# Value tiles first and by tokens, three pairs' tiles ahead of attention, three slices a step

## The reference

```python
n = rms_norm(h, attn_norm[l])
# layer 0, hybrid: 8 dilated heads (roped q, k) and 8 forgetting heads of 64
proj = n @ w_in                       # q, k, v of both kinds, and fb
logf = log_sigmoid(fb + b_f)          # the forget gate, 8 rows
o = concat(dilated_attention(rope(qa) * scale, rope(ka), va),
           forgetting_attention(qb * scale, kb, vb, logf))
h = h + o @ w_out
# layer 1, differential: 8 heads with two softmaxes and values of 128
q, k, v = split(n @ w_qkv)            # q and k roped
o = (softmax(q1 k1^T) - lam * softmax(q2 k2^T)) v
h = h + (rms_norm(o, subln_g) * (1 - lam_init)) @ w_out
```

## Time and profile before

| | before |
|---|---|
| median of 3 runs | 2503.67 us (2503.62 to 2503.73) |
| profiled execution | 2503.53 us |
| its span in the trace | 2501.6 us |
| TensorE busy | 2456.5 us (98%) |
| VectorE, ScalarE, GpSimd busy | 1568.4, 1039.2, 974.5 us |
| granted TensorE clock | 0.999 |

### The profile page before, as it was taken

The page is one execution under the profiler, slowest core; times in us unless marked ns, Lnnn a source line. Parts: engine busy times, 40 slices in busy tenths (PEclk is TensorE's granted clock), DMA queues, the critical chain, the costliest instruction groups (busy, mean ns, idle before and its releaser), DMA issues.

```text
span 2501.6 us, 33281 instructions
## 1 busy us (share of the span) xinstructions
PE 2456.5 (98%) x11238; PEld 1899.5 (76%) x11238; DVE 1568.4 (63%) x2255; ACT 1039.2 (42%) x1574; POOL 974.5 (39%) x421
## 2 busy tenths in 40 slices
PE   9999999999999999999999999999999999999998
PEld 6777888888777688888777467888877756888886
DVE  7654664777677666177678757515557876751555
ACT  5444552232344555133473654313336365431333
POOL 2232444444310044444455034444455504444443
PEclk9999999999999999999999999999999999999999
DMA  5222223232322223233222022323322202232232
GB/s 184 83 83 66 97 92 103 91 106 95 98 88 81 64 96 107 86 98 105 80 88 64 22 72 81 106 87 100 105 80 88 75 14 72 84 102 92 93 104 80
DMA packets 66510, 219.59 MB, mean 88 GB/s; under 512 B 8552, under 2 KB 8808, under 8 KB 66288
## 3 DMA queue, kind: packets, MB, share of 16 engines
q1 hardware_dynamic: 64384, 214.79, 26.9%
q10 hardware_dynamic: 2032, 3.56, 0.4%
HBM read 209.91 MB, written 2.11 MB: 85 GB/s over the span
## 4 chain that ended last, share of the span: by engine, by line
PE 87%; DVE 6%; issue 3%; ACT 3%; POOL 1%; DMA 0%; SPq 0%; DVEq 0%; POOLq 0%; ACTq 0%
PE bank_G L685 25%; PE bank_G L687 25%; PE bank_G L686 25%; PE bank_X L2442 1%; PE bank_S L1832 1%; PE bank_X L1860 1%; PE bank_O L2078 1%; PE bank_O L1846 1%; PE bank_S L2067 1%; PE bank_S L1612 1%; PE bank_S L2346 1%; PE bank_O L1622 1%; PE bank_O L2543 1%; PE bank_X L2090 0%; PE bank_X L2531 0%
## 5 line engine op out<-in xcount | busy, mean ns | idle before, releaser
L566 POOL TENSOR_TENSOR wlo<-raw,whi 128x1024 fp32r<-128x1024 f32 (+2 forms) x361 | 883.9, 2450 | 1474.3 <-ACT whi L656 1418.1
L685 PE MATMUL bank_G<-n_hi,whi 128*128 128x512 f32 x2216 | 881.2, 398 | 7.4 <-POOL wlo L566 3.2
L687 PE MATMUL bank_G<-n_hi,wlo 128*128 128x512 f32 x2216 | 863.5, 390 | 0.0
L686 PE MATMUL bank_G<-n_lo,whi 128*128 128x512 f32 x2216 | 862.9, 389 | 0.0
L656 ACT ACTIVATE whi<-raw 128x1024 fp32r<-128x1024 f32 (+2 forms) x389 | 404.3, 1041 | 676.0 <-PE bank_G L687 675.4
L685 PEld LDWEIGHTS bank_G<-n_hi,whi 128*128 128x128 f32 x2216 | 416.4, 188 | 108.9 <-issue 13.2
L687 PEld LDWEIGHTS bank_G<-n_hi,wlo 128*128 128x128 f32 x2216 | 415.9, 188 | 88.7
L686 PEld LDWEIGHTS bank_G<-n_lo,whi 128*128 128x128 f32 x2216 | 416.4, 188 | 87.4 <-issue 4.3
L685 PE MATMUL bank_G<-a_hi,whi 128*128 128x512 f32 x704 | 275.1, 391 | 0.0
L687 PE MATMUL bank_G<-a_hi,wlo 128*128 128x512 f32 x704 | 273.9, 389 | 0.0
L686 PE MATMUL bank_G<-a_lo,whi 128*128 128x512 f32 x704 | 273.9, 389 | 0.0
(11 more groups left out here) (358 smaller groups left out, 2861.6 us busy)
## 6 DMA issues: line engine op xcount, KB each, us to landing
raw<-in_w_mix_in SPq DMA_DIRECT2D x40, 512.0 KB, 3.3
raw<-in_w_hyb_in SPq DMA_DIRECT2D x25, 512.0 KB, 3.4
raw<-in_w_diff_in SPq DMA_DIRECT2D x24, 512.0 KB, 3.3
raw<-in_w_up0a SPq DMA_DIRECT2D x22, 512.0 KB, 3.3
raw<-in_w_up0b SPq DMA_DIRECT2D x22, 512.0 KB, 3.3
raw<-in_w_up1a SPq DMA_DIRECT2D x22, 512.0 KB, 3.3
raw<-in_w_up1b SPq DMA_DIRECT2D x22, 512.0 KB, 3.3
raw<-in_w_up2a SPq DMA_DIRECT2D x22, 512.0 KB, 3.3
```

Of the source, the lines that this page charges most:

```text
L566: pool.tensor_tensor(b.wlo[:, g.slot, w], b.raw[:, g.slot, w], b.whi[:, g.slot, w], ALU.subtract).then_inc(b.lo_ready, 1)
L685: pe.matmul(out, b.whi[:, g.slot, w], hi[:, hi_at + k, :], start=(k == 0), stop=False)
L686: pe.matmul(out, b.whi[:, g.slot, w], lo[:, lo_at + k, :], start=False, stop=False)
L687: mm = pe.matmul(out, b.wlo[:, g.slot, w], hi[:, hi_at + k, :], start=False, stop=(k == pieces - 1))
```

## The change

Value tiles come first in both blocks, and their products are turned around: a block of 128 tokens of `n_hi` or `n_lo` stands, 512 columns of the weights move, and the result has tokens on partitions, as attention wants it. Eight value tiles are two groups of four; each tile holds two slices of the contraction for 512 output columns, and a group accumulates over its four tiles in four banks (`value_bank`) of X, O and S. ScalarE evacuates a group into `v` (`keep_values_act`), scaled per token; for this the root is turned into a column by four small matmuls (`column`) and copied by VectorE (`keep_column_dve`). Transposes, `vst` takes, `keep_v_dve` and the posts of value tiles go. The norm's sum moves into the third tile of the hybrid block and the first of the differential one (`SUM_INSIDE`). `lead` becomes 15 (hybrid: values, q0 to k1, f, q2, k2) and 14 (differential), and `slices` 3, so that the last slice is in step 26. The forget gate's ScalarE and VectorE work moves ahead of attention. In the differential block the tile from which VectorE splits is now the 17th (before: the 15th). The host lays out the value weights to match. In `load_start` the swaps of halves of tiles 0 to 3 go, since these are value tiles now.

```diff
 def hyb_in_pe(pe, b):
-    gemm(pe, b, Index(a.g0), b.n_hi, b.n_lo, KD, lambda k: pe.wait_ge(b.nlo_ready, k + 1))
-    gemm(pe, b, Index(a.g0 + 1), b.n_hi, b.n_lo, KD, None, range(KD // 2))
-    pe.wait_ge(b.square_in, 16)
-    norm_sum(pe, b, 0)
-    gemm(pe, b, Index(a.g0 + 1), b.n_hi, b.n_lo, KD, None, range(KD // 2, KD))
+    value_tiles_pe(pe, b, a, 0, 0)
     inputs_start_pe(pe, b, a)
...
 def diff_in_pe(pe, b):
-    first_gemms_n(pe, b, ATT_DIFF.g0, 24, 2)
+    value_tiles_pe(pe, b, ATT_DIFF, 24, 2)
...
-def hyb_in_act(act, b):
+def hyb_in_act(act, b, link):
     for n in range(1, ATT_HYB.lead):
+        if n in VALUE_ENDS:
+            keep_values_act(act, b, ATT_HYB, VALUE_ENDS.index(n))
         split_hi(act, b, Index(ATT_HYB.g0 + n + 2))
+        if ATT_HYB.tiles[n - 1] == ("f", 0):
+            forget_log_act(act, b, link)
...
+VALUE_TILES, VALUE_ENDS = 8, (3, 7)
+VALUE_COLUMNS = 4 * P
+
+def value_bank(b, group, j):
+    return ((b.X, 0), (b.X, 1), (b.O, 0), (b.O, 1))[j] if group == 0 else ((b.S, 1), (b.S, 0), (b.X, 0), (b.X, 1))[j]
+
+def value_tile_pe(pe, b, a, n, nlo, between=None):
+    g, (group, t) = Index(a.g0 + n), divmod(n, 4)
+    pe.wait_ge(b.lo_ready, g.n + 1)
+    for s in range(2):
+        k, w = 2 * t + s, slice(s * VALUE_COLUMNS, (s + 1) * VALUE_COLUMNS)
+        pe.wait_ge(b.nlo_ready, nlo + k + 1)
+        for j in range(NB):
+            x, slot = value_bank(b, group, j)
+            if group == 1 and k == 0 and j >= 2:
+                pe.wait_ge(b.v_kept, VALUE_TILES * a.n + j - 1)
+            out, rows = x[:, slot, :], slice(j * P, (j + 1) * P)
+            pe.matmul(out, b.n_hi[:, k, rows], b.whi[:, g.slot, w], start=(k == 0), stop=False)
+            pe.matmul(out, b.n_lo[:, k, rows], b.whi[:, g.slot, w], start=False, stop=False)
+            mm = pe.matmul(out, b.n_hi[:, k, rows], b.wlo[:, g.slot, w], start=False, stop=(k == KD - 1))
+            if k == KD - 1 and j < NB - 1:
+                mm.then_inc(b.v_done, 1)
+        if s == 0 and between:
+            between()
+    mm.then_inc(b.gemm_done, 1)
+
+def value_tiles_pe(pe, b, a, nlo, q):
+    def squares():
+        pe.wait_ge(b.square_in, 16)
+        norm_sum(pe, b, q)
+    def column():
+        pe.wait_ge(b.rstd_ready, q + 1)
+        pe.wait_ge(b.evacuated, a.g0)
+        for j in range(NB):
+            mm = pe.matmul(b.G[:, 1, 2 * j:2 * j + 2], b.rstd[:, j * P:(j + 1) * P], b.k["ident"][:, 0:2],
+                           start=True, stop=True)
+        mm.then_inc(b.column_done, 1)
+    for n in range(VALUE_TILES):
+        value_tile_pe(pe, b, a, n, nlo, {SUM_INSIDE[a.n]: squares, 3: column}.get(n))
+
+SUM_INSIDE = (2, 0)
+
+def keep_values_act(act, b, a, group):
+    act.wait_ge(b.column_kept, a.n + 1)
+    for j in range(NB):
+        x, slot = value_bank(b, group, j)
+        if j < NB - 1:
+            act.wait_ge(b.v_done, (NB - 1) * (2 * a.n + group) + j + 1)
+        else:
+            act.wait_ge(b.gemm_done, a.g0 + VALUE_ENDS[group] + 1)
+        act.activation(b.v[:, j, group * VALUE_COLUMNS:(group + 1) * VALUE_COLUMNS], x[:, slot, :], ACT.Copy,
+                       scale=b.small[:, 8 + j:9 + j]).then_inc(b.v_kept, 1)
+
+def keep_column_dve(dve, b, a):
+    dve.wait_ge(b.column_done, a.n + 1)
+    dve.tensor_copy(b.small[:, 8:8 + NB], b.G[:, 1, 0:2 * NB].rearrange("p (j a) -> p j a", a=2)[:, :, 0]).then_inc(b.column_kept, 1)
+    dve.wait_ge(b.column_kept, a.n + 1)
+    dve.sem_inc(b.evacuated, VALUE_TILES)
...
 def in_turn():
-    tiles = [(x, o) for o in range(2) for x in "qk"]
-    for o in range(8):
-        tiles.append(("v", o))
-        if o + 2 < 8:
-            tiles += [("q", o + 2), ("k", o + 2)]
-    return tiles
-HYB_TILES = in_turn()[:4] + [("f", 0)] + in_turn()[4:]
+    return [("v", o) for o in range(8)] + [(x, o) for o in range(8) for x in "qk"]
+HYB_TILES = in_turn()[:12] + [("f", 0)] + in_turn()[12:]
...
-DVE_SPLITS = FIRST["diff_in"] + 14
+DVE_SPLITS = FIRST["diff_in"] + 16
...
-        plan_inputs(self, HYB_TILES, 4, 6, 4)
+        plan_inputs(self, HYB_TILES, 15, 3, 4)
...
-        plan_inputs(self, DIFF_TILES, 4, 6, 8)
+        plan_inputs(self, DIFF_TILES, 14, 3, 8)
```

More of the change, by code:

```diff
@@ L95 @@
 POST_HYB = 0
[L96 to L97 removed]
+POST_DIFF = POST_HYB + 64
+POST_NORM = POST_DIFF + 32
 POST_MIX = POST_NORM + 8
@@ L1423, in input_take_dve @@
     g = Index(a.g0 + n)
-    if kind == "v":
-        take_scaled(dve, b, g, b.vst[:, o % 2, :])
-    elif kind == "f":
+    if kind == "f":
         take_scaled(dve, b, g, b.ntmp[:, 0, :])
@@ L1434, in input_follow_dve, with inputs_start_dve @@
     kind, o = a.tiles[n]
[L1435 to L1438, removed]
+    rope_dve(dve, b, link, a, a.ropes.index(n), b.qk[:, qk_tile(a, kind, o), :], b.k["cos"], b.k["sin"])
 def inputs_start_pe(pe, b, a):
-    for n in range(1, a.lead):
-        if n > 1:
-            input_gemm_pe(pe, b, a, n)
-        if followed(a, n - 1):
[L1447 to L1453, removed]
+    for n in range(VALUE_TILES, a.lead):
+        input_gemm_pe(pe, b, a, n)
+    pe.wait_ge(b.v_kept, VALUE_TILES * (a.n + 1))
+def inputs_start_dve(dve, b, link, a):
+    keep_column_dve(dve, b, a)
+    for n in range(VALUE_TILES, a.lead):
+        input_take_dve(dve, b, a, n)
+        if followed(a, n - 1):
             input_follow_dve(dve, b, link, a, n - 1)
+        if n and a.tiles[n - 1] == ("f", 0):
+            forget_sums_dve(dve, b, link)
 def inputs_pe(pe, b, a, step):
@@ L1523, in followed @@
     kind, o = a.tiles[n]
-    return kind == "v" or (kind in "qk" and o < a.roped)
+    return kind in "qk" and o < a.roped
 def follows(a, step):
     return [n for n in a.follows.get(step, ()) if followed(a, n)]
-def count_posts(a, post, order):
-    order = [x for x in order if x[0] != "in" or a.tiles[x[1]][0] == "v"]
-    assert len(set(order)) == len(order) and all(kind != "v" for kind, _ in a.tiles[:a.lead - 1])
-    a.in_posts = {n: post + order.index(("in", n)) for n, (kind, _) in enumerate(a.tiles) if kind == "v"}
-    return order
 class Attention:
@@ L1731, in __init__ @@
         self.g0 = FIRST["hyb_in"]
-        plan_inputs(self, HYB_TILES, 4, 6, 4)
-        order = []
-        for step in range(self.steps):
-            if 0 <= step - self.lag < self.units:
-                order += [("att", step - self.lag, x) for x in range(2)]
-            order += [("in", n) for n in follows(self, step)]
-        order = count_posts(self, post, order)
-        self.posts = [[post + order.index(("att", u, x)) for x in range(2)] for u in range(self.units)]
+        plan_inputs(self, HYB_TILES, 15, 3, 4)
+        self.posts = [[post + 2 * u + x for x in range(2)] for u in range(self.units)]
     def unit(self, u):
@@ L1930, in hyb_attention_act @@
         inputs_act(act, b, a, step)
-        if a.tiles.index(("f", 0)) in a.ends.get(step, ()):
-            forget_log_act(act, b, link)
         o = a.fox_pair(step)
@@ L1997, in hyb_attention_dve @@
         inputs_dve(dve, b, link, a, step)
-        if a.tiles.index(("f", 0)) in a.ends.get(step - 1, ()):
-            forget_sums_dve(dve, b, link)
         if 0 <= step - a.out_step < KD:
```

40 lines of the change are left out of this document (19 added, 21 removed).

## The result

The changed kernel takes 2523.72 us (median of 4 runs, 2523.09 to 2524.73) against 2503.7 for the kernel before on the same chip (2503.62 to 2504.33): a ratio of 1.008, 95% interval 1.0068 to 1.0092. It is 20.0 us slower; the forecast was 2523.7. The profiled execution took 2524.19 us with a span of 2522.2, that is 20.6 us more span.

A forecast was written before the change was run, and what follows sets the result against it. TensorE, busy 98% of the span, was taken as the bound. Terms -7.2 + 1.8 + 2.4 + 2.1 + 2.0 + 14.5 + 5 gave +20.6, taken as 20: median 2523.7 us, range of 8 in 10 from 2506 to 2537.

The forecast's parts named there:

- Bound: Whole kernel: TensorE busy 98% of 2501.6 us, so time moves only by its work or waits put into it.
- Transposes: Value tiles: 16 groups of four transposes removed, 0.45 us net each, 7.2 us saved, upper bound 8.6.
- Same products: Value tiles: as many matmuls of 512 columns as before, whichever operand stands, so 0.
- rival of another pitch: Value products with tokens standing run at another pitch than 0.227 us, +3.5 on top for 9 ns each; chance 0.03.
- Column: Norm's column in two blocks: four small fp32 matmuls each, 0.9 us a block (0.4 to 1.6), +1.8.
- Start of the hybrid block: Third and fourth value tiles wait 1.15 and 2.4 us for low parts, together 3.6 against 1.2: +2.4.
- First attention step: Scores 1 of each block wait 2.04 us longer for masks, with three slices as cover: +2.1 and +2.0.
- Steps of the differential block: Shorter steps wait for VectorE and ScalarE: 5.7 us per eight steps, net +14.5 (bounds -1.6 and 22).
- The chain: Differential steps: in-order VectorE and ScalarE work followed through eight steps; masks and squares come late, next period at 37.7 us.
- Steps of the hybrid block: Waits of 1.1 at three 512-key steps, ropes 1.6, small ones and values 2.2: net +5 (1 to 15).
- The clock: TensorE clock falling to 1.2 GHz after long idle: given no term, as granted clock is 1.00 in all stages.
- The low end of the range: Bottom of the range of 8 in 10: 2506, described as the chain at a quarter of its price.

The follow-up runs named there:

- e6: The kernel before with one of the four transposes of each value tile, the other three token blocks left out: 2498.87 us (ratio 0.998).
- e1: The changed kernel with the norm's sum of the hybrid block inside the second value tile again: 2519.97 us (ratio 1.0066).
- e4: The changed kernel with the ropes of the last two tiles ahead of attention one step later each, both blocks: 2518.85 us (ratio 1.0059).
- e3: The changed kernel with ScalarE's root and square ahead of the step's exponentials in the differential block: 2516.07 us (ratio 1.005).
- e7: The changed kernel with every slice of the differential steps multiplied twice, 54.4 us of products added: 2562.92 us (ratio 1.0236).
- the kernel with the three edits: The changed kernel with norm's sum in the second tile, ScalarE's root and square ahead of exponentials, two ropes a step later: 2508.34 us (ratio 1.0018).
- e5: The changed kernel with four inner slices a step and 13 and 12 tiles ahead of attention: 2524.27 us (ratio 1.0079).
- e10: The changed kernel with 13 and 12 tiles ahead of attention, the remaining slices spread evenly over 27 steps: 2519.47 us (ratio 1.0062).

## Why the prediction was right

The median came out as forecast, to 0.1 us; the single terms were not that good, and errors of opposite sign met. That it came to 0.1 us is luck. By the steps of the forecast:

- **Bound.** TensorE bounds both kernels (98%). Right: VectorE lost 26 us of work, and the time rose.
- **Transposes**, -7.2: e6 speaks for 5.9 to 7.2. **Same products**, 0: the value products' pace behind the slow stretch is 0.22 to 0.23 (34.80 to 35.02); right, and the rival of another pitch falls. **Column**, +1.8: 0.8 to 0.9 a block; right.
- **Start of the hybrid block**, +2.4: the stage lost 5.6. Less the column (0.8), the clock (1.6) and a late split at 93.79 (0.4) this leaves 2.8. The wait forecast at 2.4 measured 2.12. The mechanism (root on ScalarE ahead of the fourth tile's high part) is shown by e1.
- **First attention step**, +2.1 and +2.0: two waits of 2.65 instead of 0.55 and 0.64: right, and e4 shows the rope ahead of the masks as their cause.
- **Steps of the differential block**, +14.5: the stage's +10.4 and the 3.6 of transposes make 14.0; less 2.0 for step 0 and 1.3 to 1.5 for the clock that is 10.5 to 10.7. The chain was right in each of its links, but too dear. The timeline of the three engines at the end of one head and in the next, in the changed kernel:

```profile
783.90 0.59 ACT L2171 ACTIVATE mixed<-bank_O 128x512 f32<-128x512 f32 x1
784.37 1.05 ACT L657 ACTIVATE whi<-raw 128x1024 fp32r<-128x1024 f32 x1
784.54 1.13 PE L2120 MATMUL bank_X<-mixed,const 128*128 128x512 f32 x2 [1.20 <-ACT mixed L2171]
785.46 1.23 DVE L574 TENSOR_TENSOR wlo<-raw,whi 128x1024 fp32r<-128x1024 f32 x1 [1.37 <-ACT whi L657]
785.59 1.13 PE L2089 MATMUL bank_S<-qk 64*128 64x512 f32 x4
...
790.17 0.30 PE L2111 MATMUL bank_X<-const,probs 128*128 128x128 f32 x1 [0.16 <-ACT mean L2185]
...
793.00 0.70 PE L2089 MATMUL bank_S<-qk 64*128 64x256 f32 x4 [0.44 <-DVE nmax L2228]
793.91 2.42 PE L2099 MATMUL bank_O<-pt,v 128*128 128x512 f32 x8 [0.20 <-ACT pt L2163]
...
802.82 1.13 PE L2120 MATMUL bank_X<-mixed,const 128*128 128x512 f32 x2 [1.01 <-ACT mixed L2171]
```

  ScalarE's square (783.90) stands behind its other work of the step, and the head's sum waits 1.20 for it; VectorE's split waits 1.37 for ScalarE's high part. Waits by step, forecast and measured: step 1, 1.0 and 0.6 (0.16 + 0.44); step 3, 1.35 and 1.0; step 5, 0.8 and 0.6; step 6, 0.2 for masks and none; step 7, 2.2 and 1.2. In eight steps that is 5.6 and 3.5, and two waits of 0.20 for ScalarE's copy come on top, which the forecast had apart at 0.3 each. What was mis-sized is the following of the chain. In times from the start of step 0 the releases came at 7.4, 17.2, 25.7 and 35.7 instead of 7.7, 17.4, 25.9 and 36.7: three some 0.2 to 0.3 too late, the square of step 7 a full 1.0. The time without waits was put too low, 32.0 against 36.76 - 3.9 = 32.9, which gave back half of that.
- **Steps of the hybrid block**, +5: 4.3 + 3.6 = 7.9, less 2.1 for step 0 and 1.3 to 1.5 for the clock: 4.3 to 4.5, near 5. But the working doesn't give the 5: three waits of 1.1, with 1.6 and 2.2, are 7.1, and 2.1 of them went without a reason. The three waits at steps of 512 keys were 0.41, 0.72 and 0.80. Two rows behind the second of them (VectorE's scaling of 128 columns, 0.28 us elsewhere, under GpSimd's split):

```profile
135.95 2.40 POOL L567 TENSOR_TENSOR wlo<-raw,whi 128x1024 fp32r<-128x1024 f32 x1 [7.48 <-ACT whi L657]
...
136.36 2.07 DVE L2006 TENSOR_SCALAR probs<-probs,rden 128x128 f32<-128x128 f32 x1
```

- **The clock**, no term: wrong. The forecast had itself put waits of 2.4 to 2.6 us into three places and took full clock behind them because the trace of before showed nothing else. In that trace no wait of these stages is as long (the earlier trace rows have 1.00 at most). The cost, 4.2 to 4.6 us, is almost what the differential steps were put too high by (4.0). It was itself luck: three long waits of three were followed by a slow stretch in the profiled execution, which is not so in every execution.

- **Smaller slips.** The sum gave +20.6 and 0.6 was left off without a reason; the span did rise by 20.6, and the profiled execution lies 0.5 above the median. The low end of the range, 2506, is called the chain at a quarter of its price, but a quarter of 14.5 and of 5 gives 2509.7. Only in the hybrid block does the output's first half start a step earlier; in the differential one the last slice is in step 26 in both kernels.

So the sum hit because 4.2 to 4.6 that was missing met 4.0 that was too much; the sign and most of the size stand on mechanisms that e1, e3, e4 and e7 showed one by one. No run has the turned value products with the old steps of six slices, so what they gain by themselves is known only from e6. What stays open is how to win back the last 4.6 us of the kernel with the three edits (waits for masks 3.2 and 6.9 us there, longest 1.2): spreading the slices did not take them away, and no version of the changed order came below the kernel before.

## What to carry to other kernels

Moving products ahead of a pipelined stage can remove the cover that its small chores had. Before taking it, find for each chore in an in-order queue what it stands behind, and put what TensorE waits for next ahead of what it needs later; that was worth 6.8 to 7.7 us with short steps and at most 2 with long ones. Where a change brings waits of TensorE that are longer than any in the trace of before, give the clock a term of its own (here 1.3 to 1.6 us behind 14 of 20 waits of 1.99 to 2.68 us). When a small edit seems to gain 1 to 2 us, look in the trace whether it lies where the edit is. And look whether a cure moves a VectorE operation under a split of GpSimd.

## What was unexpected of the hardware

In the changed kernel waits of 2.12, 2.65 and 2.65 us were followed by 3 to 4 us at a granted clock of 0.54 to 0.60, where matmuls of 512 columns start 0.43 us apart instead of 0.23. With waits of 1.2 us and less, as in the kernel with the three edits, the clock of these stages stayed full. Near and above 2 us both happen. The row at 105.53 above is a wait of 2.65 us in step 1 of the hybrid block with slow matmuls behind it. This is the same wait in e1, whose edit lies 80 us earlier:

```profile
101.54 0.92 PE L1859 MATMUL bank_S<-qk 64*128 64x384 f32 x4 [2.65 <-DVE nmax L1999]
102.39 0.50 PE L686 MATMUL bank_G<-n_hi,whi 128*128 128x512 f32 x1
102.72 0.40 PE L687 MATMUL bank_G<-n_lo,whi 128*128 128x512 f32 x1
```

And this is the window behind the wait of 2.12 before the fourth value tile in e3, which reads 0.54 in the changed kernel:

```profile
31.00:34.50 3.50, 3.50 (x21) 3.00 (x20) 0.00 (x0) 0.00 (x0) 2.07 (x1) 1.00 0.66 177
```

In the profiles of the changed kernel and of its versions TensorE has 20 waits of 1.99 to 2.68 us once it has begun to multiply tiles. A slow stretch follows 14 of them and not the other 6: one of 2.65 (e1), four of 2.12 or 2.13 (e3, e4, e5, e10) and one of 1.99 (e5; in the same profile another of 1.99 is followed by one). It never follows a single wait of 1.8 us or less; in e5, at 244.61, one of 1.29 followed by 0.35 and 0.41 was enough (0.56 from 245.3 to 249). So the length of the wait alone doesn't decide, and what else does is open. It is not the program either: e1's five executions have clocks of 0.998 at 2519.1 to 2520.0 us and of 0.996 at 2521.6 and 2521.8.

The Trainium skill, "TensorE: Matmul & The Clock Gate", Part 1, has the clock fall from 2.4 to 1.2 GHz after long idle. The trace agrees on the two levels (0.43 us is about twice 0.227), and 2.12 us of idle were enough in the changed kernel, though not in four other profiles. A slow stretch isn't all loss: taking three away gave 2.85 us of the 4.6, since the other engines use it to catch up.
